# The projection matmuls beside each attention unit, issued in one run behind the scores

## The reference, cut to what matters

```python
def attend(q, k, v, scale):
    s = jnp.einsum('bqhgd,bkhd->bhgqk', qg, k).astype(jnp.float32) * scale
    p = jax.nn.softmax(s, axis=-1).astype(v.dtype)
    o = jnp.einsum('bhgqk,bkhd->bqhgd', p, v)
...
def diff_attend(q1, q2, k1, k2, v, lam, scale):
    p1 = jax.nn.softmax(jnp.einsum('bqhd,bkhd->bhqk', q1, k1).astype(jnp.float32) * scale, axis=-1)
    p2 = jax.nn.softmax(jnp.einsum('bqhd,bkhd->bhqk', q2, k2).astype(jnp.float32) * scale, axis=-1)
    p = (p1 - lam * p2).astype(v.dtype)
    return jnp.einsum('bhqk,bkhd->bqhd', p, v)
```

## Time and profile before

| | |
|---|---|
| runs | 4441.81, 4454.0, 4456.94 us, median 4454.0 us |
| profiled execution | 4448.05 us, span 4446.4 us |
| TensorE busy | 4171.1 us, 94% of the span |
| DVE, ACT, POOL busy | 29%, 16%, 6% |
| chain that ended last | PE 88%, DVE 6%, DMA 3% |

### The profile page before, as it was taken

How to read it: one execution, slowest core, us unless ns; L and a number is a source line. 1 busy time by engine, 2 the same in 40 slices (tenths; PEclk the granted TensorE clock), 3 DMA queues, 4 the chain that set the end, 5 groups by cost and what they waited for, 6 DMA issues and landing times.

```text
span 4446.4 us, 51347 instructions
## 1 busy us (share of the span) xinstructions
PE 4171.1 (94%) x21570; PEld 2930.6 (66%) x21570; DVE 1290.2 (29%) x2777; ACT 728.6 (16%) x1553; POOL 288.6 (6%) x326
## 2 busy tenths in 40 slices
PE   5999999999999998899999999988988988899998
PEld 3447545544446676776776857776775777788887
DVE  1000344620023222130034135555455555100001
ACT  2100122310011221120022012222222222000000
POOL 0000000000000003100000001210220122000000
PEclk9999999999999999999999999989999978799999
DMA  8433322233434336853212420011001000344443
GB/s 342 163 136 129 114 95 95 86 153 140 151 112 155 136 119 158 230 209 133 76 59 105 147 84 21 20 40 40 21 20 40 31 1 1 104 143 160 152 158 126
DMA packets 77504, 489.58 MB, mean 110 GB/s; under 512 B 10480, under 2 KB 14576, under 8 KB 23648
## 3 DMA queue, kind: packets, MB, share of 16 engines
q1 hardware_dynamic: 70560, 462.45, 29.0%
q0 software_dynamic: 6720, 23.78, 2.0%
HBM read 482.00 MB, written 4.19 MB: 109 GB/s over the span
## 4 chain that ended last, share of the span: by engine, by line
PE 88%; DVE 6%; DMA 3%; issue 2%; ACT 1%; POOL 0%; DVEq 0%; ACTq 0%; POOLq 0%
PE ps L930 47%; PE ps L1031 7%; PE ps L924 7%; PE ps L1137 3%; PE ps L1122 3%; PE ps L869 3%; PE ps L990 3%; PE ps L1134 3%; PE ps L1009 2%; PE ps L927 2%; DMA w<-in_wi 1%; PE ps L1000 1%; PE ps L1162 1%; DVE zone L2023 1%; PE ps L1174 1%
## 5 line engine op out<-in xcount | busy, mean ns | idle before, releaser
L930 PE MATMUL ps<-h,w 128*128 128x256 f32 (+1 forms) x4992 | 1554.4, 463 | 51.7 <-DMA w<-in_wi 34.6
L930 PEld LDWEIGHTS ps<-h,w 128*128 128x128 f32 x4992 | 940.4, 193 | 509.2 <-issue 409.8
L930 PE MATMUL ps<-y,w 128*128 128x256 f32 (+1 forms) x1792 | 507.8, 441 | 1.7 <-DMA w<-in_wo 1.7
L930 PEld LDWEIGHTS ps<-y,w 128*128 128x128 f32 x1792 | 338.0, 190 | 156.4 <-issue 121.9
L1031 PE MATMUL ps<-h,w 128*128 128x256 f32 (+1 forms) x1024 | 370.3, 501 | 1.3 <-issue 1.3
L924 PE MATMUL ps<-w,h 128*128 128x256 f32 x1280 | 278.6, 379 | 0.0
L924 PEld LDWEIGHTS ps<-w,h 128*128 128x128 f32 x1280 | 243.0, 190 | 38.5 <-issue 6.1
L1031 PEld LDWEIGHTS ps<-h,w 128*128 128x128 f32 x1024 | 182.2, 189 | 111.8 <-issue 91.3
L817 POOL TENSOR_TENSOR zone<-zone 128x512 f32<-128x512 f32 x160 | 203.1, 1272 | 641.5 <-DVE zone L2019 352.7
L869 PE MATMUL ps<-w,zone 128*32 128x256 f32 x2304 | 150.0, 403 | 25.3 <-DVE zone L2083 11.7
L1137 PE MATMUL ps<-zone 128*128 128x128 f32 x1280 | 168.3, 275 | 0.0
(11 more groups left out here) (306 smaller groups left out, 3887.0 us busy)
## 6 DMA issues: line engine op xcount, KB each, us to landing
w<-in_wm SPq DMA_DIRECT2D x144, 1024.0 KB, 8.0
w<-in_we SPq DMA_DIRECT2D x52, 1024.0 KB, 5.0
w<-in_w SPq DMA_DIRECT2D x48, 1024.0 KB, 5.0
w<-in_wmg SPq DMA_DIRECT2D x48, 1024.0 KB, 5.0
w<-in_wi SPq DMA_DIRECT2D x34, 1024.0 KB, 5.1
w<-in_wo SPq DMA_DIRECT2D x32, 1024.0 KB, 5.0
w<-in_wrw SPq DMA_DIRECT2D x32, 1024.0 KB, 5.0
w<-in_wbr SPq DMA_DIRECT2D x48, 512.0 KB, 4.3
```

Of the source, the lines that this page charges most:

```text
L930: last = mm(pass_psum(s, q), rows[:, n * P:(n + 1) * P], src[k], start=(k == 0), stop=(k == s.kt - 1))
```

## The change

The change is in TensorE's `attend`. The matmuls of `pulls[i]` were pulled in three shares: one behind the scores, one behind the transposes, one behind the output matmuls. Now all of them are pulled behind the scores. Nothing else is changed, nor the order on any other engine.

```diff
                 for i in range(n + 3):
-                    share = [pulls[i] // 3, (pulls[i] + 1) // 3, (pulls[i] + 2) // 3]
                     if i < n:
...
                         last.then_inc(s_sc, 1)
                     also(i)
-                    run(beside, share[2])
+                    run(beside, pulls[i])
                     if 2 <= i <= n + 1:
...
                         last.then_inc(s_tp, 1)
-                    run(beside, share[1])
                     if i >= 3:
...
                         last.then_inc(s_o, 1)
-                    run(beside, share[0])
                 run(beside)
```

## The result

| | before | after |
|---|---|---|
| median of 8 runs | 4451.76 us | 4466.58 us |
| lowest and highest | 4441.81, 4456.94 us | 4462.02, 4470.56 us |
| profiled execution | 4448.05 us | 4464.26 us |
| TensorE busy | 4171.1 us | 4163.7 us |

The kernel became slower: ratio after to before 1.0036, 95% interval 1.0025 to 1.0047, that is 16 us (11 to 21) of 4451. (The ratios of this document are those of the means, so they differ a little from those of the medians.) The two profiled executions differ by 16.2 us.

The account below looks back on a forecast made before the run. It took TensorE's chain of work to bound the kernel, with no wait to win in stages a and n. Terms 23.6 - 4.8 + 1 - 1 = +18.8 us on a level of 4451 gave 4470 us, range 4455 to 4485.

Parts of the forecast that it names:

- The loop in stage a: Stage a: next scores wait for exponentials, themselves released by transposes, with only output matmuls left as cover; +23.6 us.
- the four waits of a head: Stage a: scores wait 0.79, 0.35, 0.78 and 1.22 us for q = 0 to 3, 3.14 us a head.
- The seams of n: Stage n: outputs and scores touch, two gaps become one, 0.17 us saved in 28 units; -4.8 us, between 0 and -7.
- Stage b: Stage b: sums of squares wait longer for DVE's mean, against the 2.19 us wait for ACT's copy; +1 us.
- sign of being wrong: Stage b or the transfers behind d moving by more than 3 us would show the prediction wrong.
- the clock rival: Stage a: the clock falls after the longest new wait once a head, 12 us on top, 4482 us; chance 0.12.
- the end of d: End of stage d: next weights asked for about 1 us earlier, POOL's transfers later; -1 us, between -3 and 0.
- Stage c: Stage c: no wait on exponentials and no seam gain; length kept within 1 us.
- Hidden anyway: Stage a pays nothing, exponentials released otherwise or short enough; 4446 us, no measurable change; chance 0.08.
- fewer seams pay: Every unit loses two seams between small and large groups, at 0.20 us each 27 us faster, 4424 us; chance 0.04.

Follow-up runs that it names:

- three buffers: Against the changed kernel, a third buffer for the probabilities in stage a, same order on TensorE; median 4442.9 us of 12 runs, ratio 0.9984 to before.

## Why the prediction was right, point by point

**The loop in stage a** was right in mechanism and size: 23.6 us forecast, 23.57 us by the gaps, 24.4 us by the stretch. (One bound has a slip: 0.1 us more for the release and 0.1 us for ACT's start in 29 waits add 5.8 us, so the upper bound should have been 29.4 us and not 27.) The means of the four waits of a head and that of unit 2 (1.66 us) agree to 0.01 us. That the free buffer is what ACT waits for, and that this is the cause, is shown by the three buffers: the same order without that dependency loses nothing. The other 0.8 us of the stretch are the eight iterations with matmuls of the modulation, 4 x 0.15 + 4 x 0.05, the same with two and with three buffers. The prediction had nothing for them: it took it that "in a the seam of scores and full tiles exists before and after".

**The seams of n**: -4.8 us forecast, -5.7 measured from the stage's first scores to the gate behind it (148.09 and 142.38 us). The term was mis-sized: "I take 0.17, the mean of the two that it replaces". The direct seam costs 0.13 to 0.14 us, no more than the cheaper of the two, so 0.20 us is saved in each of 28 units, 5.6 us.

**Stage b** was wrong in sign: +1 us forecast, -3.8 measured, outside the bounds of -2 to +3, and by more than the 3 us that the prediction itself had named as a sign of being wrong. The step that failed is the balance of the longer waits of L962 against the wait for ACT. These came to +0.9 us in all, where it had 0.3 to 0.7 us for each of five units, and -0.9 us. Left out were two things: that the half-speed stretch behind that wait, which the clock rival had priced at 1.5 us, would go (1.7 us), and that the argument on weights asked for earlier, made only for the end of d, holds at the end of b as well (1.5 us).

**Stage c**: nothing forecast, -1.0 us measured. At its end the sum of squares waited for ACT's square of the last pass. TensorE before:

```profile
1570.00 1.96 PE L962 MATMUL ps<-zone,mats 128*128 128x512 f32 x4 [0.96 <-ACT zone L1433]
```

and after, without a wait:

```profile
1590.69 1.14 PE L1007 MATMUL ps<-zone 128*128 128x128 f32 x8
1591.79 1.96 PE L962 MATMUL ps<-zone,mats 128*128 128x512 f32 x4
```

The last projection now ends ahead of the output matmuls, which cover the chain over ACT. It is the same effect as in a with the sign turned. In every kernel that leaves c as it was that wait is there, and in none with its order changed. The length of c alone would say less: with a alone changed it was 167.67 us, 1.7 us less than before, because the half speed behind the first scores of c was missing.

**The end of d** cannot be judged. The waits for weights (`in_wi`) are shorter in most kernels with the new order in d, 24.1 to 33.8 us against 31.9 to 38.5 us in the five profiles without it, but another wait came. TensorE's waits from d to n, before:

```profile
PE ps L930 <- DMA w<-in_wi: 34.6, 4, 12.8
```

and after:

```profile
PE ps L930 <- DMA w<-in_wi: 26.9, 4, 11.5
...
PE ps L869 <- DVE modc L1707: 6.2, 1, 6.2
```

The second wait is in every kernel in which the order of d is changed (6.1 to 10.3 us) and in none of the four experiments that leave d as it was, so it comes from the order in d; how, the runs don't show. A size of its own the term does not get: over all profiles this stretch took 637.6 to 654.5 us, and 637.6 and 640.5 where nothing was changed but the order in n behind it. A term of 1 us can't be seen in that.

**The rivals.** The granted clock in stage a stayed at 0.99, with waits of up to 1.66 us in 29 of 32 units, so that rival is out, and with it the rule of the Trainium skill, TensorE: Matmul & The Clock Gate, section "A second HAM failure mode: psum-queue depth-cycling", as far as idles of this length in this rhythm are concerned. "Hidden anyway" is refuted by the 29 waits, "fewer seams pay" by stage a with three buffers, where the scores wait for nothing and no iteration got shorter but by the clock.

**The sum.** Forecast +18.8 us, measured +16.2 in the profiles and +16 by the ratio. The errors are +0.8 (a), +2.1 (ahead of a, where the order is unchanged: over the eleven profiles this part took 488.3 to 492.1 us, so it is chance), -4.8 (b), -1.0 (c), +1.6 (d), -1.4 (n to the end), together -2.7. That the total came so close is in part luck: the errors that add time (4.5 us, 2.1 of them chance) offset most of those that take it (7.2 us). The level of 4451 us taken for the kernel before is what its 23 runs gave, 4451.21.

## What to carry to other kernels

When independent matmuls are used as cover, write down for each in-order engine the chain that leaves TensorE and comes back (here the last transpose, the exponentials, the next scores: 0.31 us and ACT's 1.02 or 1.45 us), and count what lies between its two ends after the move; the total amount of filler says nothing. Filler is best placed inside the tightest chain, here between transposes and scores, and one more buffer takes the chain away altogether. Where the tile changes its shape, let the two small shapes touch and do not put a full-size tile between them: that won 0.20 us a unit in n and lost 0.15 us in four iterations of a. And look at the last iteration of a stage by itself: the order there decides when the next weights are asked for.

## What the runs showed of the hardware

A direct change from a tile of 128 rows by 64 columns to one of 64 rows costs 0.13 to 0.14 us, against 0.34 for the two changes by way of a full tile. The Trainium skill, TensorEngine Tiling (Array Packing), section "Key Properties", says that switching the mode needs the array drained; the rows agree that each change costs, and show that the price depends on the pair: 0.14, 0.20, 0.13.

The granted clock did not fall behind waits of 0.35 to 1.66 us in 29 of the 32 units of a, nor behind one of 1.33 us in b. Behind the wait of 2.19 us in b it fell to 0.50 in the kernel before and not at all with stage a alone changed, with the same matmuls around it, 1.7 us apart. In a, a wait of 2.20 us ahead of the first scores was followed by half speed in ten of the eleven profiles and by full speed with three buffers, 1.70 us apart. So a wait of this length may cost 1.7 us more or nothing, and before a difference of that size between two profiles is put down to an edit, their granted clocks should be compared.
